# Loading the experts' down weights through GpSimd's DMA queue in a hybrid-layer kernel

## The reference, cut to what matters

```
logits = u @ w_router + b_router              # 32 experts
top_val, top_idx = lax.top_k(logits, 4); gates = softmax(top_val)
for every expert e, on the rows routed to it:
    gu   = xb @ w_gu[e] + b_gu[e]             # w_gu[e]:   1024 x 2048
    gate = minimum(gu[:, :1024], 7);  lin = clip(gu[:, 1024:], -7, 7)
    act  = (lin + 1) * gate * sigmoid(1.702 * gate)
    y    = act @ w_down[e] + b_down[e]        # w_down[e]: 1024 x 1024
h = h + sum of gate-weighted y;  out = rmsnorm(h) * g_final
```

## Time and profile before

| | us |
|---|---|
| median of 3 runs (lowest, highest) | 1145.69 (1145.49, 1146.31) |
| time of the profiled execution | 1146.64 |
| its span | 1144.9 |
| TensorE busy | 1089.3 (95%) |
| VectorE busy | 345.3 (30%) |
| ScalarE busy | 192.9 (17%) |
| GpSimd busy | 14.2 (1%) |
| data moved | 425.30 MB, mean 371 GB/s |
| granted TensorE clock, mean | 0.984 |

### The profile page before, as it was taken

The page is one execution under the profiler, slowest core; times in us unless marked ns, Lnnn a source line. Parts: engine busy times, 40 slices in busy tenths (PEclk is TensorE's granted clock), DMA queues, the critical chain, the costliest instruction groups (busy, mean ns, idle before and its releaser), DMA issues.

```text
span 1144.9 us, 13663 instructions
## 1 busy us (share of the span) xinstructions
PE 1089.3 (95%) x5256; PEld 455.4 (40%) x5256; DVE 345.3 (30%) x639; ACT 192.9 (17%) x306; POOL 14.2 (1%) x39
## 2 busy tenths in 40 slices
PE   6999899999999999999999999999999999999995
PEld 5757744333333333333333333333333333333332
DVE  3756123212222222222222222222222222222233
ACT  2335232111111111111111111111111111111112
POOL 3000000000000000000000000000000000000000
PEclk9989898999999999999999999999999999999999
DMA  9561072899999999999999999999999999999994
GB/s 308 192 220 42 3 294 111 301 415 426 426 426 426 426 427 426 426 427 426 428 425 429 423 429 424 428 426 425 426 426 427 423 427 425 428 425 427 425 424 190
DMA packets 54063, 425.30 MB, mean 371 GB/s; under 512 B 7392, under 2 KB 14167, under 8 KB 21275
## 3 DMA queue, kind: packets, MB, share of 16 engines
q1 hardware_dynamic: 53368, 424.67, 89.6%
q0 software_dynamic: 512, 0.26, 0.1%
q10 hardware_dynamic: 162, 0.09, 0.0%
HBM read 422.69 MB, written 2.35 MB: 371 GB/s over the span
## 4 chain that ended last, share of the span: by engine, by line
DMA 51%; PE 44%; DVE 2%; ACT 2%; SPq 1%; issue 1%; DVEq 0%
DMA raw<-in_w_gu 47%; PE ps L1315 20%; PE ps L1329 6%; PE ps L1062 4%; PE ps L1336 2%; PE ps L1295 2%; DMA raw<-in_w_down 2%; PE ps L1196 2%; PE ps L1085 1%; PE ps L1043 1%; PE ps L1358 1%; SPq L265 1%; PE ps L1302 1%; DMA wv<-v_rows 1%; DMA yacc<-in_x_prompt 1%
## 5 line engine op out<-in xcount | busy, mean ns | idle before, releaser
L1315 PE MATMUL ps<-raw,xT 128*64 128x512 f32 x2048 | 467.6, 601 | 22.9 <-DMA raw<-in_w_gu 22.2
L1315 PEld LDWEIGHTS ps<-raw,xT 128*64 128x64 f32 x2048 | 140.3, 138 | 316.5 <-issue 270.1
L1329 PE MATMUL ps<-raw,actT 128*64 128x512 f32 x992 | 218.4, 592 | 0.0
L989 DVE TENSOR_TENSOR yacc<-ps,yacc 128x1024 f32<-128x1024 f32 x96 | 111.7, 1217 | 161.8 <-PE ps L1336 146.5
L963 DVE TENSOR_TENSOR hS<-ps,bguT 128x512 f32<-128x512 f32 x64 | 41.2, 686 | 371.3 <-PE ps L1358 371.3
L1329 PEld LDWEIGHTS ps<-raw,actT 128*64 128x64 f32 x992 | 71.1, 137 | 141.3 <-issue 140.5
L584 ACT ACTIVATE xr<-ps 128x512 f32<-128x512 f32 x32 | 19.1, 597 | 410.6 <-PE ps L1295 406.9
L1336 PE MATMUL ps<-yS,GT 64*128 64x512 f32 x372 | 88.2, 606 | 0.0
L1295 PE MATMUL ps<-u,sel 128*64 128x512 f32 x372 | 85.1, 592 | 0.0
L953 DVE TENSOR_TENSOR sel<-slot_no,pos 128x192 f32<-128x192 f32 x32 | 11.5, 358 | 145.9 <-PE ps L1295 144.2
L1336 PEld LDWEIGHTS ps<-yS,GT 64*128 64x128 f32 x372 | 33.4, 186 | 54.3 <-issue 54.3
(11 more groups left out here) (298 smaller groups left out, 565.2 us busy)
## 6 DMA issues: line engine op xcount, KB each, us to landing
raw<-in_w_gu SPq DMA_DIRECT2D x128, 2048.0 KB, 23.4
raw<-in_w_down SPq DMA_DIRECT2D x128, 1024.0 KB, 24.6
wv<-in_w_in SPq DMA_DIRECT2D x3, 2048.0 KB, 13.1
raw<-in_w_in SPq DMA_DIRECT2D x2, 2048.0 KB, 20.6
wv<-in_w_out SPq DMA_DIRECT2D x1, 4096.0 KB, 13.1
wv<-in_state_gla SPq DMA_DIRECT2D x8, 128.0 KB, 2.3
wv<-v_rows SPq DMA_DIRECT2D x4, 256.0 KB, 5.3
out_gla_s<-wv SPq DMA_DIRECT2D x8, 128.0 KB
```

What stands on the lines that cost most here:

```text
L989: dve.tensor_tensor(dst, ps[:, PAIR[c]:PAIR[c] + 2, :], dst, ALU.add).then_inc(sem("added"), 1)
L1315: last = pe.matmul(ps[S * w:S * w + S, n, :], xT[:, k % 4, k // 4, :], raw[:, k, col:col + 512], start=(k == 0), stop=(k == KD - 1))
L1329: last = pe.matmul(ps[S * w:S * w + S, bank, :], acts[:, k, :], weights[:, col:col + 512], start=(k == 0), stop=(k == KD - 1))
```

## The change

GpSimd's program gets the down loads of experts 0 to 30, with the same waits, sizes, addresses and semaphores that SP's had. SP keeps all gate and linear loads, and the down loads of expert 31 at the end. Nothing changes on the other engines.

```
-                e = e_of(i)
-                if p in GU:
-                    src = A["w_gu"][0, bass.ds(e, 1), p * P:(p + 2) * P, :]...
-                    load(raw[:, p:p + 2, :], src, f"piece_in{p}")
-                else:
-                    r = (p - 8) * 2 * P
-                    src = A["w_down"][0, bass.ds(e, 1), r:r + 2 * P, :]...
-                    load(raw[:, p, :].rearrange("p (k n) -> p k n", k=2), src, f"piece_in{p}")
-            for p in (*GU[1:], *DN):
+                src = A["w_gu"][0, bass.ds(e_of(i), 1), p * P:(p + 2) * P, :]...
+                load(raw[:, p:p + 2, :], src, f"piece_in{p}")
+            for p in GU[1:]:
                 piece(p, 0, first=True)
...
             def round_of(i):
                 for p in GU:
                     piece(p, i)
-                for p in DN:
-                    piece(p, i - 1)
...
+            def down_rows_in(i, first=False):            # GpSimd
+                for p in DN:
+                    if not first:
+                        pool.wait_ge(sem(f"used{p}"), i)
+                    r = (p - 8) * 2 * P
+                    src = A["w_down"][0, bass.ds(e_of(i), 1), r:r + 2 * P, :]...
+                    pool.dma_start(raw[:, p, :]..., src).then_inc(sem(f"piece_in{p}"), 16)
+            pool.wait_ge(sem("mix_ready"), MA + 1)
+            pool.wait_ge(sem("out_mix"), 16 * (1 + NB + 5))
+            down_rows_in(0, first=True)
+            with pool.Fori(2, SPLIT) as i:
+                down_rows_in(i - 1)
+            pool.wait_ge(sem("flag_ready"), 1)
+            over = pool.value_load(flag[0:1, 0:1], min_val=0, max_val=1)
+            with pool.If(over):
+                with pool.Fori(SPLIT, SPLIT + NV - NE) as i:
+                    down_rows_in(i - 1)
+            more = over * (NV - NE)
+            with pool.Fori(SPLIT, NE) as i:
+                down_rows_in(i + more - 1)
```

More of the change, by code:

```diff
@@ L318, in piece @@
                     sp.wait_ge(sem(f"used{p}"), i)
-                e = e_of(i)
-                if p in GU:
-                    src = A["w_gu"][0, bass.ds(e, 1), p * P:(p + 2) * P, :].rearrange("e (p k) n -> p (e k) n", p=P)
-                    load(raw[:, p:p + 2, :], src, f"piece_in{p}")
-                else:
-                    r = (p - 8) * 2 * P
-                    src = A["w_down"][0, bass.ds(e, 1), r:r + 2 * P, :].rearrange("e (p k) n -> p (e k) n", p=P)
-                    load(raw[:, p, :].rearrange("p (k n) -> p k n", k=2), src, f"piece_in{p}")
-            for p in (*GU[1:], *DN):
+                src = A["w_gu"][0, bass.ds(e_of(i), 1), p * P:(p + 2) * P, :].rearrange("e (p k) n -> p (e k) n", p=P)
+                load(raw[:, p:p + 2, :], src, f"piece_in{p}")
+            for p in GU[1:]:
                 piece(p, 0, first=True)
@@ L434, in _ @@
                                pattern=[[1, P]], channel_multiplier=-1).then_inc(sem("tri_ready"), 1)
+            def down_rows_in(i, first=False):
[3 more added lines that the diff above has]
+                    r = (p - 8) * 2 * P
+                    src = A["w_down"][0, bass.ds(e_of(i), 1), r:r + 2 * P, :].rearrange("e (p k) n -> p (e k) n", p=P)
+                    pool.dma_start(raw[:, p, :].rearrange("p (k n) -> p k n", k=2), src).then_inc(sem(f"piece_in{p}"), 16)
+            pool.wait_ge(sem("mix_ready"), MA + 1)
[11 more added lines that the diff above has]
+                down_rows_in(i + more - 1)
         @block.scalar
```

## The result

The changed kernel takes 1149.62 us (median of 20 runs, 1145.61 to 1153.87); the kernel before, run beside it, 1145.38 us (20 runs, 1140.59 to 1147.46). The ratio over all these runs is 1.0044, with a 95% interval of 1.0029 to 1.0059: slower by 5.0 us, 3.3 to 6.8 (the medians alone lie 4.2 us apart). Forecast were 6.4 us.

The account below looks back on a forecast made before the run. The full DMA queue at 426 GB/s was taken to bound the kernel, its end set by the stream's end plus TensorE work left. Bytes, issue and start 0, order 6.4: 1145.7 + 6.4 = 1152.1 us, range 1145 to 1161.

Parts of the forecast that it names:

- Bytes and rate: Expert stream: same bytes, engines busy throughout, 426 GB/s, 29.5 us rounds, last landing about 1127; no change.
- rate rivals (slower, faster): Stream rate falls: 1157 to 1187 us, chance 0.11; two queues keep engines fuller: 1139.3 at 432 GB/s, chance 0.10.
- 34 us: In the falling-rate rival: 34 ns on top of each 8 KB down packet, 1.1 us a round, put near 0.
- Issue: GpSimd's four added issues a round: 0.58 us each, 2.3 us on an engine empty there; taken as 0.
- Start: Expert 0's loads: two queues bring the same bytes by the same time; 0, covered by 16 us.
- Overtaking: GpSimd's down loads land ahead of SP's earlier gate loads; only moves waits mid-kernel, costs 6.4 us at the end.
- Step 3: End: with dn(30) ahead, gu(31, 6) lands at 1117.5 and expert 31's down work ends at 1137.5, 6.5 us later.
- the same 6.5 us: End, queues sharing one to two: dn(30) and gu(31, 6) end together at 1117.5, costing 6.5 us.
- if TensorE is not behind already: Condition on the 6.4 to 6.5 us; bound above, TensorE before all of dn(30) at stream's end: 13.0 us.
- down weights late: Rival, chance 0.10: GpSimd's queue gets less than its third, TensorE waits for dn every round; 6.4 to 13 us.
- the forecast's own: Order lost, rate kept, at the stream's end: 1152.1 us, own range 1149 to 1156, chance 0.58.
- if the clock fell in longer waits: Sign in the profile after that the prediction is wrong; no place or size given.

Follow-up runs that it names:

- rows of 8 KB: Changed kernel with each 2 MB gate load as two loads of 1 MB; ratio to the kernel before 1.0146 (1.0114 to 1.0179).
- every other piece: Kernel before with gu 2, gu 6, dn 9, dn 11 moved to GpSimd: 1.0049; with GpSimd's expert 0 loads behind the router's weights: 1.0005.
- kernel with dn(1) in its place: Kernel before with dn(0) loaded into the unused 4 MB buffer while DMA engines stand still, dn(1) in its old place; ratio 0.9986 (0.9967 to 1.0005).
- the mended kernel with all loads by GpSimd: Against the all-GpSimd kernel: expert 0's big loads wait for router weights and biases, last norm's weights follow dn(31) on GpSimd; ratio to before 1.0011.

## Why the prediction was right, and where its steps were not

*Bytes and rate, right.* 426 GB/s throughout, rounds of 29.5 us, the stream's end at about 1127 us. Both rate rivals (slower, faster) find nothing in the changed kernel. (In the first of them 1152.1 and 34 us are 1186, not 1187; nothing hangs on it.)

*Issue, right.* 0.541 us for a 1 MB load (0.58 us taken from 16 KB ones); with all loads on GpSimd the kernel is the same within what can be told.

*Start, right by luck of size.* The router's small loads were not named as what expert 0's loads could overtake. In the changed kernel VectorE waited 11.3 us for them instead of 5.9, and that was hidden (45.9 us against 46.1). With 10 MB instead of 4 on GpSimd it wasn't.

*Overtaking, half right.* The queues share by packets, one row each, as the early stretch suggested, and the kernels with other sharing move the waits as they should. But only the first three down loads of the round shown land sooner than the 24.6 us that were the median before (11.6 us for the first); the last takes 27.4 us. The gate loads, said to land no sooner than before, land after 15.3 us instead of 23.4.

*Where the time is lost, wrong in its place.* Step 3 has TensorE wait for gu(31, 6) at 1117.5. It didn't: in the changed kernel no matmul waits for a gate load, in any round. The queues share one to two, and for that case the prediction says that dn(30) and gu(31, 6) end together, "the same 6.5 us", "if TensorE is not behind already". It was behind already: with just a third of the rate while both queues have work, dn(i, 11) is the load that is waited for, and the last wait that counts is at dn(29, 11), 38.6 us before the end of the down matmuls. That is the rival "down weights late" in its mechanism, which had a chance of 0.10 against 0.58 for the forecast's own. Its size of 6.4 to 13 us fits the 7.3 us of the profile at its low end and lies above the 5.0 (3.3 to 6.8) of the times. One thing in it is off: q0 gets just its third, not less. Step 3's own case was seen with rows of 8 KB.

*The clock.* The prediction would be wrong, it says, "if the clock fell in longer waits". It did fall behind the waits of 2.3 to 2.8 us, at 332 us (0.57 from 332 to 336 us) and four times from 774 us on. The one that counts is the last, 1.4 of the 7.3 us, and the sum has no term for it.

*The size.* 6.4 us forecast, 5.0 measured. Since the sum was made at another place, its nearness is partly luck. What it had right is the bound from which it was made: the stream's end does not move, so the loss is TensorE's work behind it, 11.6 us instead of 3.65 in the profile. In the two-queue kernels whose end was read it is between nothing more (every other piece) and 8.1 us more (rows of 8 KB).

## What to carry to other kernels

Here one queue fed an engine in the order of use, and its stream was the bound. A second queue added no rate (426 GB/s in both); it only let loads pass each other, and what that cost was paid once, at the end, as work left over when the stream was done. Waits that the old order has at the end are given back first (here 3.4 us at dn(31)), so compare the lag with them. If a second queue is wanted for the sake of its issuing engine, give each queue a like share of every round, in order (the "every other piece" kernel), or go back to one queue for the last rounds. And look which small, urgent loads on the first queue will now meet the second one's large ones: here the router's biases were waited for up to 10 us longer.

## What was not expected of the hardware

- The sharing goes by packets, not by bytes, while both queues have work: 158 against 152 packets and 2.33 against 1.11 MB in 8 us with rows of 16 and 8 KB, 234 against 234 and 1.71 against 1.65 MB with rows of 8 KB in both.
- Rows of 8 KB throughout moved 422 GB/s, rows of 16 KB with a third of the bytes in 8 KB rows 426 (one kernel with the former, and it also has more loads).
- A wait of 2.65 us ahead of the first half of dn(31) left the granted clock at 1.00 in the kernel before (16 matmuls in 3.66 us). In the kernel with dn(1) in its place the same wait, 2.66 us, was followed by 0.56 in the next 3 us, near the lower level of 1.2 GHz, and the 16 matmuls took 5.35 us; so it was in the mended kernel with all loads by GpSimd, behind 2.65 us. So 1.7 us between two profiles can come with waits of the same length, and these runs don't show what decides it.
- The mixing half, the same work in all kernels, reached the router's load between 142.7 and 148.4 us. Why was not found.
